# The second mixer of a three-block network: first queries' product put ahead of the keys', and the rotations and turns that follow it reordered

## The reference, cut to what matters

```python
def dsa_mixer(hn, positions, w_in, w_out):
    proj = hn @ w_in                                   # 1024 x 1860
    q, k, v, qi, ki, wi = jnp.split(proj, ODD_SPLITS, axis=-1)
    q = rope(q.reshape(B, S, 8, 128), positions)
    k = rope(k.reshape(B, S, 2, 128), positions)
    qi = rope(qi.reshape(B, S, 4, 64), positions)
    ki = rope(ki.reshape(B, S, 1, 64), positions)[:, :, 0]
    # index scores: sum over 4 heads of wi * relu(qi . ki); the 64 best keys of each query are kept
    # attention of 8 query heads in 2 groups over the kept keys, then @ w_out
    o = dsa_attention(q, k, v, qi, ki, wi)
    return o @ w_out
```

## Time and profile before

| | us |
|---|---|
| median of 3 runs | 1502.72 (1502.15 to 1503.18) |
| the profiled execution | 1503.14 |
| its span from the first to the last instruction | 1501.2 |
| PE busy | 1478.0 (98%) |
| DVE busy | 871.9 (58%) |
| ACT busy | 710.5 (47%) |
| GpSimd busy | 92.6 (6%) |

### The profile page before, as it was taken

How to read it: one execution, slowest core, us unless ns; L and a number is a source line. 1 busy time by engine, 2 the same in 40 slices (tenths; PEclk the granted TensorE clock), 3 DMA queues, 4 the chain that set the end, 5 groups by cost and what they waited for, 6 DMA issues and landing times.

```text
span 1501.2 us, 16932 instructions
## 1 busy us (share of the span) xinstructions
PE 1478.0 (98%) x7067; PEld 1231.6 (82%) x7067; DVE 871.9 (58%) x1024; ACT 710.5 (47%) x837; POOL 92.6 (6%) x107
## 2 busy tenths in 40 slices
PE   9999999999999999999999999999999889999999
PEld 6888888888888888888788888888888768888887
DVE  6465466654546545468665454755447777665543
ACT  6444355644434444444464434534336756454432
POOL 0000003000000000008000000000000440000000
PEclk9999999999999999999999999999999989999999
DMA  9755453465555655554456555655555352555552
GB/s 318 235 175 182 148 204 113 140 224 175 191 168 183 210 184 180 169 177 139 140 184 195 186 182 176 195 189 195 182 166 192 120 168 85 196 193 187 181 182 71
DMA packets 145106, 265.66 MB, mean 177 GB/s; under 512 B 7134, under 2 KB 27318, under 8 KB 144774
## 3 DMA queue, kind: packets, MB, share of 16 engines
q1 hardware_dynamic: 143174, 259.11, 52.8%
q0 software_dynamic: 1136, 4.35, 0.9%
q10 hardware_dynamic: 720, 1.11, 0.2%
HBM read 263.52 MB, written 1.05 MB: 176 GB/s over the span
## 4 chain that ended last, share of the span: by engine, by line
PE 91%; DVE 3%; POOL 2%; ACT 2%; DMA 1%; issue 0%; POOLq 0%; ACTq 0%; SPq 0%; DVEq 0%
PE ps L534 28%; PE ps L536 28%; PE ps L535 28%; PE ps L582 2%; DVE wlo L1516 1%; POOL d_tmp L2084 1%; PE ps L565 1%; DMA raw<-in_ffn_wi 1%; PE ps L942 1%; PE ps L743 1%; PE ps L647 1%; PE ps L683 1%; POOL d_q L2086 0%; ACT whi L1126 0%; PE ps L650 0%
## 5 line engine op out<-in xcount | busy, mean ns | idle before, releaser
L1516 DVE TENSOR_TENSOR wlo<-raw,whi 128x2048 fp32r<-128x2048 f32 (+4 forms) x268 | 568.0, 2124 | 424.1 <-ACT whi L1126 423.8
L1126 ACT CAST whi<-raw 128x2048 fp32r<-128x2048 f32 (+4 forms) x268 | 473.7, 1770 | 446.2 <-PE ps L536 441.4
L534 PE MATMUL ps<-whi,xt_hi 128*128 128x512 f32 (+3 forms) x1376 | 533.3, 388 | 1.1 <-DVE xt_lo L1530 0.7
L536 PE MATMUL ps<-whi,xt_lo 128*128 128x512 f32 (+3 forms) x1376 | 527.0, 383 | 0.0
L535 PE MATMUL ps<-wlo,xt_hi 128*128 128x512 f32 (+3 forms) x1376 | 526.8, 383 | 0.0
L534 PEld LDWEIGHTS ps<-whi,xt_hi 128*128 128x128 f32 x1376 | 258.7, 188 | 51.9 <-DVE xt_lo L1530 1.4
L536 PEld LDWEIGHTS ps<-whi,xt_lo 128*128 128x128 f32 x1376 | 258.5, 188 | 50.3
L535 PEld LDWEIGHTS ps<-wlo,xt_hi 128*128 128x128 f32 x1376 | 258.8, 188 | 47.8
L534 PE MATMUL ps<-whi,yt_hi 128*128 128x512 f32 (+3 forms) x108 | 43.4, 402 | 7.5 <-DVE wlo L1516 5.4
L1152 ACT ACTIVATE junk<-X 128x512 f32<-128x512 f32 x40 | 25.4, 635 | 43.4 <-DVE X L1571 40.0
L536 PE MATMUL ps<-whi,yt_lo 128*128 128x512 f32 (+3 forms) x108 | 42.0, 389 | 0.0
(11 more groups left out here) (386 smaller groups left out, 1614.0 us busy)
## 6 DMA issues: line engine op xcount, KB each, us to landing
raw<-in_ffn_wi SPq DMA_DIRECT2D x79, 1024.0 KB, 5.1
raw<-in_ffn_wo SPq DMA_DIRECT2D x40, 1024.0 KB, 5.0
raw<-in_ffn_w_gate SPq DMA_DIRECT2D x20, 1024.0 KB, 5.0
raw<-in_ffn_w_up SPq DMA_DIRECT2D x20, 1024.0 KB, 5.0
raw<-in_ffn_w_down SPq DMA_DIRECT2D x20, 1024.0 KB, 4.9
raw<-in_w_in SPq DMA_DIRECT2D x14, 1024.0 KB, 5.2
raw<-in_ffn_wi SPq DMA_DIRECT2D x16, 512.0 KB, 4.6
raw<-in_even_w_in SPq DMA_DIRECT2D x6, 1024.0 KB, 5.2
```

What stands on the lines that cost most here:

```text
L534: e.matmul(o, h, hi_w, start=i == 0 and j == 0, stop=False)
L536: t = e.matmul(o, l, hi_w, start=False, stop=(end or (v == len(plan) - 2 and tt == 1)) and j == nk - 1)
L1126: e.copy(whi[0:n, v % SPLIT, c], raw[0:n, v % RAW, c]).then_inc(s_hi.mark(*[(v, j) for j in js]), 1)
L1516: e.tensor_tensor(wlo[0:n, v % SPLIT, c], raw[0:n, v % RAW, c], whi[0:n, v % SPLIT, c].bitcast(F32), ALU.subtract).then_inc(s_lo.mark(*[(v ...
```

## The change

The weight blocks, PE's program, ACT's, DVE's and GpSimd's are reordered in the second mixer. No instruction of compute is added or removed; every operation keeps its size.

- In the plan, `dq0`'s first block stands where `dk`'s did, between the two blocks of `di`, and both blocks of `dk` come behind `dq0`.
- PE: after `turn_x` two k-tiles of `dq0`, then `di`'s second block, three k-tiles of `dq0` (the last two of its first block, the first of its second), `index_turn`, a k-tile, `index_scores`, the last two k-tiles, both blocks of `dk`, `dq1` with `query_turn(0)` in its second block, and `key_turn` after two k-tiles of `dv`. `head_scores(0)` comes after `dv`'s first block and no longer in its middle.
- ACT: scales `dq0`, then `dk`; copies the turned first queries, scales `dq1`, and copies the turned keys last.
- DVE: one `unit()` is moved from before the index part's rotation to between the first two calls of `select()`.
- GpSimd: rotates `dq0`, `dk`, `dq1` and no longer `dk`, `dq0`, `dq1`.

```diff
-                + together(di, dk) + both(dq0) + both(dq1) + both(dv) + together(*d_out)
+                + together(di, dq0) + both(dk) + both(dq1) + both(dv) + together(*d_out)
...
                 steps(di, 0)
                 turn_x("b1", 1)
-                steps(dk, 0)
+                steps(dq0, 0, 0, 2)
                 steps(di, 1)
                 give(di.name, s_act["di"])
+                steps(dq0, 0, 2)
+                steps(dq0, 1, 0, 1)
+                index_turn()
+                steps(dq0, 1, 1, 2)
+                index_scores()
+                steps(dq0, 1, 2)
+                give(dq0.name, s_act["dq", 0])
+                steps(dk, 0)
                 steps(dk, 1)
                 give(dk.name, s_act["dk"])
-                steps(dq0, 0, 0, 2)
-                index_turn()
-                steps(dq0, 0, 2, 3)
-                index_scores()
-                steps(dq0, 0, 3)
-                steps(dq0, 1, 0, 2)
+                steps(dq1, 0)
+                steps(dq1, 1, 0, 2)
+                query_turn(0)
+                steps(dq1, 1, 2)
+                give(dq1.name, s_act["dq", 1])
+                steps(dv, 0, 0, 2)
                 key_turn()
-                steps(dq0, 1, 2)
-                give(dq0.name, s_act["dq", 0])
-                steps(dq1, 0)
-                steps(dq1, 1)
-                give(dq1.name, s_act["dq", 1])
-                query_turn(0)
-                steps(dv, 0, 0, 2)
+                steps(dv, 0, 2)
                 head_scores(0)
-                steps(dv, 0, 2)
                 scored(dat, 0)
                 steps(dv, 1)
...
                     rotate(Iq[:, tt, 0:320].rearrange("p (h b f) -> p h b f", h=5, b=2), 5, 0, 2, 32, room, tt, ("index", tt))
...
                 select()
+                unit()
                 select()
```

More of the change, by code:

```diff
@@ L1320, in dsa @@
                 unit()
-                unit()
                 q.wait_ge(*s_dve["rs", "b1"])
@@ L1324, in dsa @@
                 unit()
-                scaled("dk", lambda tt: dK[:, tt, :], dk, RS)
                 unit()
@@ L1333, in dsa @@
                                  ACT.Relu).then_inc(s_act.mark(("relu", tt)), 1)
+                scaled(("dq", 0), lambda tt: dQ[:, tt, 0:512], dq0, RS)
                 unit()
-                q.wait_ge(*s_turn["dkt"])
-                e.copy(dKT[:, :, :], Pair("dkt").flat[:, 0:512].rearrange("p (g t) -> p g t", g=2)).then_inc(s_act.mark("dkt"), 1)
-                scaled(("dq", 0), lambda tt: dQ[:, tt, 0:512], dq0, RS)
+                unit()
+                scaled("dk", lambda tt: dK[:, tt, :], dk, RS)
                 unit()
@@ L1341, in dsa @@
                 unit()
+                query_turn(0)
                 scaled(("dq", 1), lambda tt: dQ[:, tt, 512:1024], dq1, RS)
-                query_turn(0)
+                q.wait_ge(*s_turn["dkt"])
+                e.copy(dKT[:, :, :], Pair("dkt").flat[:, 0:512].rearrange("p (g t) -> p g t", g=2)).then_inc(s_act.mark("dkt"), 1)
                 unit()
@@ L2121, in dsa @@
             def dsa():
+                q.wait_ge(*s_act["dq", 0])
+                for tt in range(2):
+                    rotate(dQ[:, tt, 0:512].rearrange("p (h b f) -> p h b f", h=4, b=2), 4, 0, 1, 64, room2, tt, ("dq", 0) if tt else ("dq", 0, 0))
                 q.wait_ge(*s_act["dk"])
@@ L2124, in dsa @@
                     rotate(dK[:, tt, :].rearrange("p (h b f) -> p h b f", h=2, b=2), 2, 0, 1, 64, room2, tt, ("dk", tt))
-                q.wait_ge(*s_act["dq", 0])
-                for tt in range(2):
-                    rotate(dQ[:, tt, 0:512].rearrange("p (h b f) -> p h b f", h=4, b=2), 4, 0, 1, 64, room2, tt, ("dq", 0) if tt else ("dq", 0, 0))
                 q.wait_ge(*s_act["dq", 1])
```

## The result

| | before | after |
|---|---|---|
| median, us | 1502.72 (1502.15 to 1503.85, 5 runs) | 1509.14 (1508.44 to 1510.69, 5 runs) |
| ratio | | 1.0043 (95%: 1.0029 to 1.0058) |
| profiled execution, and its span | 1503.14, 1501.2 | 1508.44, 1504.9 |

A forecast was written before the change was run, and what follows sets the result against it. PE, busy 98% of the span, bounds the kernel. A 2.2 us shift at full clock plus 3.4 for two slow stretches makes 5.6: profiled 1503.14 to 1508.7, median 0.4 lower, 1508.3 us (range 1503.0 to 1511.0).

The forecast's parts named there:

- Entry wait: At the second mixer's entry PE waits for xt_lo behind the wider block: 2.05 us, bounds 1.7 and 2.3.
- Index turn: PE arrives at 678.3, the index part's rotation ends at 678.6: a wait of 0.3 us.
- First queries at GpSimd: GpSimd starts rotating the first queries at 688.4, 3.9 us sooner than before.
- GpSimd, the term that decides: GpSimd's rotations in the second mixer: first queries done at 701.0, keys at 709.0 (8.0 us), second queries at 717.6.
- Key wait: At the key turn PE, there at 706.1, waits 2.9 us for keys ready at 709.0.
- From the scores to normalised scores: Group 0's softmax chain, from the scores' start at 710.9 to normalised scores at 720.2: 9.3 us, before 10.1.
- my bound of 0.5 more: The 9.3 us softmax chain grows by 0.5 us if the subtraction ahead of it waits for GpSimd.
- Shift at full clock: Scores of group 1 start at 721.5 against 719.28: 2.2 us later, today's figure already holding a slow stretch of 1.7.
- The clock: two falls, one of before won: Half-clock stretches behind the key wait and the last wait, 3.4 us together; none behind the entry; today's 1.7 us won.
- My price of 1.7 a fall: Each stretch in which PE's granted clock falls to 0.50 was taken to cost 1.7 us.
- keys in time: Rival: keys rotated at 704.1, before PE needs them, so not slower: 1500.0 or 1499.5 us; chance 0.07.
- One slow stretch: Rival: one fall of the clock in place of two, 1506.6 us; chance 0.20.

The follow-up runs named there:

- the split entry: Changed kernel with the first queries' first block rounded and subtracted in two halves, one ahead of the add to X, one behind the turn of X: 1506.18 us, ratio 1.0021.
- the first experiment: Kernel before with GpSimd rotating the keys behind the first queries, the key turn moved into dv, plan and entry unchanged: 1509.2 us, ratio 1.0044.
- the filled kernel: Changed kernel with useless products on PE, four ahead of the key turn and five ahead of the first probabilities' turn: 1506.12 us, ratio 1.0025.
- the two filled kernels: Useless products in PE's waits, in the changed kernel (1506.12 us) and in the kernel before, four ahead of each query turn (1501.83 us).
- first trace: Profiled execution of the changed kernel's first series of five runs: 1508.44 us, span 1504.9; the series' median is 1509.14.
- second trace: Profiled execution of the unaltered changed kernel when measured again in nine runs: 1509.76 us, span 1507.0.
- second series: The changed kernel measured again, unaltered, in nine runs: median 1507.69 us, ratio 1.0032.
- keys behind: Kernel before with GpSimd's key rotation put behind the first queries and the key turn moved into dv, nothing else of the change: 1509.2 us, ratio 1.0044.

## Why the prediction was right

It gave 1508.3 (1503.0 to 1511.0); the medians are 1509.14 and 1507.69. By its own steps, with the times of the profiled execution less its offset of 0.57:

- **Entry wait, 2.05 (1.7 to 2.3): right, 1.77.** The row at the start of the third mixer was the right one to borrow. That it reaches the end is shown by the split entry.
- **Index turn, 0.3: 0.24.**
- **First queries at GpSimd, 688.4: 688.6.**
- **GpSimd, the term that decides: right.** The first group is done at 701.2 (701.0), the keys at 708.5 (709.0). The keys took 7.3 us with two 1024-wide subtractions beside them; I took 8.0 between bounds of 6.2 and 8.7. My lower bound of 6.2 was taken from a row that was not undisturbed: the second four multiplies of the keys took 2.21 before, beside DVE's index sums, and 1.69 in the first experiment with DVE idle; so the keys take some 5.1 undisturbed, and DVE added 2.2. The page's rule (the Trainium skill, SBUF — State Buffer, section "Who interferes with whom") would have given 7.2 here; the rows agree with it: each four multiplies of queries beside a 2048-wide subtraction took 4.89 and 4.91, undisturbed 2.81.
- **Key wait, 2.9: too long, 2.0.** PE came at 706.6 and not at 706.1, the keys 0.5 sooner. The sum of it, the start of the scores of group 0, is 711.0 against 710.9.
- **From the scores to normalised scores, 9.3: too short.** It took 10.5 us in the trace with the slow stretch (the scores at half clock cost 1.2 of it), 10.0 in the filled kernel at full clock: there DVE's 2048-wide subtraction took 3.0 us beside GpSimd. That is the case of my bound of 0.5 more, by 0.7.
- **Shift at full clock.** From "2.2 us" plus the 1.7 that today's figure holds, 3.9. Measured between the two filled kernels, neither with a slow stretch: 57.0 - 52.9 = 4.1. Of it 1.9 is the entry (57.0 against 55.1 with the entry split), the other 2.2 what GpSimd's queue and the places of the turns make of it; these two were not told apart at full clock.
- **The clock: two falls, one of before won: the number is near, the places are right only in part, and some of that is luck.** The first trace shows one fall, behind the key wait; the second has two, behind the entry wait, which I left out, and behind the last. That is 5.2 us at the scores of group 1. The spans differ by 1507.0 - 1501.2 = 5.8, where I had 5.6; of the rest 0.3 lies ahead of the turn of X and 0.2 behind the scores. My price of 1.7 a fall was too high: 0.9 to 1.5 was measured. In the second trace the fall behind the entry wait, priced at nothing, stood in for the one behind the key wait. Filling the waits wins 1.6 to 3.0 us of the median (from 1507.69 or 1509.14 to 1506.12), or 1.1 to 3.0 if each series is held against its own kernel before. With the entry split it is 3.6 together, more than either edit alone against the same series: entry and clock are separate terms. The rule on idle gaps (the Trainium skill, TensorE: Matmul & The Clock Gate, section "Why this matters for your kernels") would have no fall here and 1504.9; the falls behind 1.8 and 2.0 us speak against it.

What stays open: which of three waits is followed by a fall differs from execution to execution, with waits of the same length at two of them (1.77 and 2.02 in both traces), and no run tells why. In the profiled executions other waits shift with it, so a slow stretch is worth 0.9 us at the scores of group 1 (57.9 against 57.0, changed and filled kernel) where DVE's chain covers a part of it, and 1.5 where nothing does. The third mixer, whose program is the same in both kernels, has a slow stretch of 10.2 us in the trace of before and of some 6.8 us in both traces of the changed kernel, so single spans differ by such stretches too. And 1.6 us of the first profiled execution's time lies outside its span (3.5 against 1.9 before), which no view shows.

Of the rivals, "keys in time" fell at what spoke against it: the keys stand behind 12.6 us of queries. "One slow stretch", 1506.6, is near the four quickest of the second series (1505.8 to 1507.4), though no trace tells how many falls these had.

## What to carry to other kernels

Before moving work up on an engine, write down that engine's queue with its releasers: here the queries were rotated sooner, and the keys, needed by the same consumer, were pushed behind them; a consumer of two things is served by the later one. A wide block put ahead of an add on which a norm depends delays the norm by what the wider block takes longer on ACT and DVE both (here a wait of 1.8 us), and splitting it was enough to win that back. And price a wait with what the clock may take behind it: products of no use in an unavoidable wait kept the clock here and left 0.3 to 0.4 us of most of the waits; they won 1.1 to 3.0 us in the changed kernel and 1.4 us in the kernel before, the latter at the edge of what can be told apart.

## What the runs showed of the hardware that was not expected

- The granted clock fell to 0.50 for about 3.4 us behind idle times of PE of 1.8 and 2.0 us, and behind waits of the same two lengths in another execution of the same program it did not, nor behind 2.9 us in the first profiled one. In each of the five kernels with useless products in the waits it was 1.00 from 660 to 750.
- A slow stretch is not always 3.4 us. With the key wait of 2.8 us inside it, the clock stayed down for 10.2 us (keys behind). In the kernel with the keys on DVE it was down for 6.8 us, from 716.8 on, which is 1.0 us before the wait of 4.1 us ended.
- The disturbance between DVE and GpSimd goes both ways. GpSimd's 128x512 add took 1.30 us alone and 3.19 beside a 2048-wide subtraction that had begun before it (the subtraction at 711.91, the add at 712.13); DVE's 2048-wide subtraction took 2.28 alone and 3.01 beside an add of GpSimd that had begun before it (filled waits: the add at 715.57, the subtraction at 715.98). In both cases the one that began first kept its own time, 2.28 and 1.27.
